# An FFN's norm statistics taken one pair later, x loaded in eight pieces on two queues, and the layer loop written out

## The reference

```
for l in range(2):
    x = x + 0.5 * swiglu(rmsnorm(x, g1[l]), w_ffn1_in[l], w_ffn1_out[l])
    x = x + mixing_sublayer(rmsnorm(x, g2[l]), ...)            # retention and forgetting attention
    x = x + 0.5 * swiglu(rmsnorm(x, g3[l]), w_ffn2_in[l], w_ffn2_out[l])
rmsnorm(x, g) = x * rsqrt(mean(x*x over the 1024 channels) + 1e-6) * g
swiglu(h)     = (silu(h @ w_in[:, :2816]) * (h @ w_in[:, 2816:])) @ w_out
```

## Time and profile before

| what | value |
|---|---|
| median of the three runs | 3042.85 us (3035.99 to 3043.49) |
| profiled execution | 3036.15 us, its span 3034.4 us |
| mean granted TensorE clock | 0.989 of full speed |
| busy: TensorE matmul, VectorE, ScalarE | 97%, 48%, 33% of the span |
| chain that ended last | TensorE 93%, VectorE 4%, ScalarE 2%, issue 1% |

### The profile page before, as it was taken

The page is one execution under the profiler, slowest core; times in us unless marked ns, Lnnn a source line. Parts: engine busy times, 40 slices in busy tenths (PEclk is TensorE's granted clock), DMA queues, the critical chain, the costliest instruction groups (busy, mean ns, idle before and its releaser), DMA issues.

```text
span 3034.4 us, 36777 instructions
## 1 busy us (share of the span) xinstructions
PE 2953.1 (97%) x13442; PEld 2378.1 (78%) x13442; DVE 1446.1 (48%) x2087; ACT 998.1 (33%) x1546; POOL 0.2 (0%) x4
## 2 busy tenths in 40 slices
PE   8999999999999999999999999999998999999996
PEld 6888887778888887888887778888887877777775
DVE  6443345555544425444255554544435445455555
ACT  3222223333322322222123233332223345434453
POOL 0000000000000000000000000000000000000000
PEclk9999999999999999999999999999999999999998
DMA  4323232212233232323232212323332121122111
GB/s 139 91 89 103 90 115 78 62 56 83 90 97 97 90 104 84 97 91 101 92 116 77 70 55 76 97 84 96 97 98 83 63 69 42 49 84 70 43 42 56
DMA packets 69368, 251.67 MB, mean 83 GB/s; under 512 B 7696, under 2 KB 7824, under 8 KB 69008
## 3 DMA queue, kind: packets, MB, share of 16 engines
q1 hardware_dynamic: 68400, 246.46, 25.8%
q10 hardware_dynamic: 864, 3.79, 0.3%
HBM read 248.13 MB, written 2.10 MB: 82 GB/s over the span
## 4 chain that ended last, share of the span: by engine, by line
PE 93%; DVE 4%; ACT 2%; issue 1%; DMA 0%; DVEq 0%; SPq 0%; ACTq 0%
PE bank L465 26%; PE bank L467 26%; PE bank L466 26%; PE bank L573 1%; PE bank L575 1%; PE bank L574 1%; PE bank L628 1%; PE bank L638 1%; PE bank L818 1%; PE bank L829 1%; PE bank L695 1%; PE bank L804 1%; PE bank L748 1%; PE bank L775 1%; PE bank L760 1%
## 5 line engine op out<-in xcount | busy, mean ns | idle before, releaser
L465 PE MATMUL bank<-xh,wh 128*128 128x512 f32 x2384 | 956.5, 401 | 16.0 <-DVE start_d L2071 9.5
L466 PE MATMUL bank<-xl,wh 128*128 128x512 f32 x2384 | 945.4, 397 | 0.0
L467 PE MATMUL bank<-xh,wl 128*128 128x512 f32 x2384 | 945.0, 396 | 0.0
L1461 DVE TENSOR_TENSOR wl<-raw,wh 128x1024 fp32r<-128x1024 f32 x460 | 561.2, 1221 | 303.6 <-ACT wh L1068 302.9
L1068 ACT ACTIVATE wh<-raw 128x1024 fp32r<-128x1024 f32 x460 | 483.4, 1052 | 398.3 <-PE bank L467 251.9
L465 PEld LDWEIGHTS bank<-xh,wh 128*128 128x128 f32 x2384 | 450.3, 189 | 127.2 <-issue 18.7
L467 PEld LDWEIGHTS bank<-xh,wl 128*128 128x128 f32 x2384 | 449.9, 189 | 109.0
L466 PEld LDWEIGHTS bank<-xl,wh 128*128 128x128 f32 x2384 | 450.3, 189 | 106.5 <-issue 1.9
L1509 DVE TENSOR_TENSOR ta<-bank,rstd 128x512 f32<-128x512 f32 x88 | 60.9, 692 | 463.3 <-PE bank L467 460.7
L467 PE MATMUL bank<-uh,wl 128*128 (+1 forms) x704 | 277.4, 394 | 0.0
L466 PE MATMUL bank<-ul,wh 128*128 (+1 forms) x704 | 276.0, 392 | 0.0
(11 more groups left out here) (355 smaller groups left out, 2832.6 us busy)
## 6 DMA issues: line engine op xcount, KB each, us to landing
raw<-stream SPq DMA_DIRECT2D x460, 512.0 KB, 3.5
x<-x_t SPq DMA_DIRECT2D x4, 512.0 KB, 8.1
dec<-decay ACTq DMA_DIRECT2D x2, 1024.0 KB, 6.3
out<-x SPq DMA_DIRECT2D x8, 256.0 KB, 2.0
rp<-rope ACTq DMA_DIRECT2D x2, 512.0 KB, 7.6
cst<-const SPq DMA_DIRECT2D x1, 708.5 KB, 10.8
ffraw<-ff_w ACTq DMA_DIRECT2D x2, 316.0 KB, 9.8
posi<-pos SPq DMA_DIRECT2D x1, 256.0 KB, 10.4
```

Source lines behind the costliest of these rows:

```text
L465: pe.matmul(o, wh[:, s, c], rhs_h, start=first, stop=False)
L466: pe.matmul(o, wh[:, s, c], rhs_l, start=False, stop=False)
L467: return pe.matmul(o, wl[:, s, c], rhs_h, start=False, stop=last)
L1461: dve.tensor_tensor(wl[:, at.slot, :], raw[:, at.raw, :], wh[:, at.slot, :].bitcast(F32), ALU.subtract).then_inc(split_lo, 1)
```

## The change

1. Start: `vecs` is loaded first, then panel 0; x comes in eight loads, tiles 2, 4, 6 on SyncE's queue and 0, 1, 3, 5, 7 on ScalarE's. ScalarE makes `xh` of the first norm, VectorE only `xl`.
2. Every FFN: `chain_col` moves into the middle of the second pair, `chain_bc` into the middle of the third. Pairs 3 and 4 are written out before TensorE's loop. Panels 4 and 5 are split in `norm_chain` (`highs`, `lows`), after `diag` and ahead of the copy of `rstd`; the first pair then splits none and the second only panel 6.
3. The first pair's banks are 4, 5 in both FFNs; the mixing sublayer's output uses banks 2, 3 instead of 2, 5.
4. The loop over the two layers is written out on TensorE, ScalarE and VectorE.

```diff
         def _(sp):
+            sp.dma_start(vecs[:], vec).then_inc(vec_in, 16)
             sp.dma_start(raw[:, 0, :], stream[0]).then_inc(raw_in[0], 16)
-            sp.dma_start(vecs[:], vec).then_inc(vec_in, 16)
-            for i in range(X_PARTS):
-                d = slice(i * KD // X_PARTS, (i + 1) * KD // X_PARTS)
-                sp.dma_start(x[:, d, :], x_in[:, d, :]).then_inc(x_part[i], 16)
-                if i == 1:
+            for d in (2, 4, 6):
+                sp.dma_start(x[:, d, :], x_in[:, d, :]).then_inc(x_part[d], 16)
+                if d == 4:
                     sp.dma_start(raw[:, 1, :], stream[1]).then_inc(raw_in[1], 16)
...
-                    if first:
+                    if first and j < 2:
                         pe.wait_ge(*resid.at(n * KD + (1 if j == 0 else KD - 1), "X"))
-                    else:
+                    elif not first:
                         pe.wait_ge(*fin.at(it - 2, "B"))
...
-                        if first and j == 1 and half == 0:
-                            chain_bc(n, 7)
-                    if first and j == 0:
-                        pe.wait_ge(const_in, 16)
-                        chain_col(n, 6)
+                        if first and half == 0:
+                            if j == 1:
+                                pe.wait_ge(const_in, 16)
+                                chain_col(n, 6)
+                            elif j == 2:
+                                chain_bc(n, 7)
...
-            with pe.Fori(0, DEPTH) as l:
+            for l in range(DEPTH):
...
+            for d in (0, 1, 3, 5, 7):
+                act.dma_start(x[:, d, :], x_in[:, d, :]).then_inc(x_part[d], 16)
             act.wait_ge(memsets, 1)
             act.activation(start_a[:], eps[:], ACT.Copy).then_inc(rg_act.sem, 1)
             high(At(0, 0), True)
-            squares(0, lambda d: d in (1, 6) and high(At(0, 1 + d // 4), True))
-            high(At(0, LEAD), True)
+            act.wait_ge(vec_in, 16)
+            for d in range(KD):
+                act.wait_ge(x_part[d], 16)
+                act.activation(xh[:, d, :], x[:, d, :], ACT.Copy, scale=vecs[:, d:d + 1]).then_inc(start_h, 1)
+                if d == 3:
+                    high(At(0, 1), True)
+            squares(0, lambda d: d in (1, 5) and high(At(0, 2 + d // 4), True))
...
                 chain_std(l * 3 + 2, 6)
+                highs(p0 + AT_FFN2, (1, 2))
...
             for d in range(KD):
                 add_squares(0, d)
-                if d == 6:
-                    low(At(0, 2))
-            low(At(0, LEAD))
+                if d in (1, 5):
+                    low(At(0, 2 + d // 4))
...
-                norm_chain(n2, 7)
-                ffn_in(l * 2 + 1, n2, p0 + AT_FFN2, FIRST_BANKS[1])
+                norm_chain(n2, 7, lambda: lows(p0 + AT_FFN2, (1, 2)))
+                ffn_in(l * 2 + 1, n2, p0 + AT_FFN2)
```

More of the change, by code:

```diff
@@ L312, in build @@
         panel_done = sem("panel_done")
-        x_part = [sem(f"x_part{i}") for i in range(X_PARTS)]
+        x_part = [sem(f"x_part{i}") for i in range(KD)]
         vec_in, const_in, pos_in = sem("vec_in"), sem("const_in"), sem("pos_in")
@@ L516, in pair @@
                         last.then_inc(panel_done, 1)
-                        if first and j == 1 and half == 0:
-                            chain_bc(n, 7)
-                    if first and j == 0:
-                        pe.wait_ge(const_in, 16)
-                        chain_col(n, 6)
-                for j in range(2):
-                    pair(j, idx + 2 * j, None, True)
-                with pe.Fori(1, KF // 2) as i:
+                        if first and half == 0:
[4 more added lines that the diff above has]
+                                chain_bc(n, 7)
+                for j in range(4):
+                    pair(j, idx + 2 * j, f * KF + j, j < 3)
+                with pe.Fori(2, KF // 2) as i:
                     for j in range(2):
@@ L1068, in high, with highs @@
                 act.activation(wh[:, at.slot, :], raw[:, at.raw, :], ACT.Copy).then_inc(split_hi, 1)
+            def highs(at, tiles):
+                for i in tiles:
+                    high(at + i + LEAD)
             def squares(n, after=None):
@@ L1084, in ffn_in, with pair @@
             def ffn_in(f, idx):
-                def pair(j, at, first):
+                def pair(j, at, splits):
                     it = f * KF + j
-                    if not first:
+                    if splits > 1:
                         high(at + LEAD)
@@ L1415, in _ @@
             act.activation(cos2[64:112, :], turn[64:112, :], ACT.Sin).then_inc(trig_act.sem, 1)
-            with act.Fori(0, DEPTH) as l:
+            for l in range(DEPTH):
                 p0 = At(l * (LAYER1 // SLOTS), 0)
@@ L1495, in diagonal, with lows @@
                                   ALU.mult).then_inc(st.sem, 1)
+            def lows(at, tiles):
+                for i in tiles:
+                    low(at + i + LEAD)
             def norm_chain(n, b, between=None):
@@ L1509, in scaled, with ffn_in, pair @@
                 dve.tensor_tensor(dst, src, rstd[:], ALU.mult).then_inc(st.sem, 1)
-            def ffn_in(f, n, idx, first_banks):
-                def pair(j, a, b, at, first=False):
+            def ffn_in(f, n, idx):
+                def pair(j, a, b, at, splits):
                     it = f * KF + j
-                    if not first:
+                    if splits > 1:
                         low(at + LEAD)
@@ L1521, in pair @@
                     dve.tensor_tensor(u32[:], sa[:], tb[:], ALU.mult).then_inc(fin.sem, 1)
-                    low(at + 1 + LEAD)
+                    if splits:
+                        low(at + 1 + LEAD)
                     dve.wait_ge(*fin_act.at(it, "UH"))
@@ L1527, in ffn_in @@
                 dve.wait_ge(*chain.at(n, "RB"))
[L1528 to L1529 removed]
+                pair(0, *(bank[i] for i in FIRST_BANKS), idx, 0)
+                pair(1, bank[2], bank[3], idx + 2, 1)
                 with dve.Fori(1, KF // 2) as i:
                     for q in range(2):
[L1532 removed]
+                        pair(i * 2 + q, bank[2 * q], bank[2 * q + 1], (idx + 2 * q).fours(i), 2)
             def ffn_out(f, n, idx):
@@ L2084, in _, with meanwhile @@
             reduced("s", ang, 0.0, "A")
-            norm_chain(0, 7, lambda: reduced("c", turn, 0.25, "s6"))
+            def meanwhile():
+                reduced("c", turn, 0.25, "s6")
+                lows(At(0, 0), (1, 2))
+            norm_chain(0, 7, meanwhile)
             dve.tensor_copy(ident16[:], ident).then_inc(mask_set, 1)
             dve.tensor_copy(masks[:], cst[:, C_CAUSAL:C_KEEP]).then_inc(mask_set, 1)
-            with dve.Fori(0, DEPTH) as l:
+            for l in range(DEPTH):
                 p0 = At(l * (LAYER1 // SLOTS), 0)
-                ffn_in(l * 2, l * 3, p0, FIRST_BANKS[0])
+                ffn_in(l * 2, l * 3, p0)
                 n = l * 3 + 1
```

36 lines of the change are left out of this document (21 added, 15 removed).

## The result

The changed kernel takes 3052.82 us (median of six runs, 3050.95 to 3054.19), the kernel before, with three more runs beside it, 3040.84 us (six runs, 3035.99 to 3043.49). The ratio is 1.0041, 95% interval 1.0028 to 1.0054: slower by 12 us, with 8.5 as the lower end. The profiled execution took 3050.95 us, its span 3049.2 us, against 3036.15 and 3034.4.

What follows compares the result with a forecast made beforehand. TensorE, busy 97% of the span, bounds the kernel. Start -1.8, layer 1's first FFN +0.9, two second FFNs +2.5 each, two clock falls +4.4 sum to +8.5: 3051 us on base 3042.85, range 3039 to 3060.

Steps and rivals of the forecast that it cites:

- the later FFNs: FFNs after the program's first: +2.5 us for each layer's second FFN, +0.9 for layer 1's first.
- the start: Program start through the first FFN: column-sum wait goes, third and fourth pairs wait; fourth pair at 52.3 against 54.09, -1.8 us.
- the clock: TensorE's clock falls behind two of the four longer new waits, 2.2 us each: +4.4 us, bounds 0 and +11.
- The fourth-pair wait: Layer 0's second FFN: TensorE's fourth pair waits 2.5 us for panel 6's split, queued behind the later broadcast and rstd copy.
- the sign: Trace sign of being right: each FFN's fourth pair's first matmul waits 2.4 to 2.6 us for `wl`, not a bank.
- Layer 1's first FFN: There the late `ta` stops mattering and the new fourth-pair wait does: fourth pair at 1213.40 against 1212.50, +0.9 us.
- rival 3: All FFNs: no fourth-pair wait; start wins 7.5 and up to 1.4, layer 1's first FFN 1.5; -10.4 us, 3032; 5%.
- The splits ahead of `rstd`: Splitting panels 4 and 5 between `diag` and the copy costs VectorE 2.4 us, hidden by 3 in layer 0's second FFN.
- Rival 1: Whole program: TensorE's clock holds through all the new waits; +4.1 us, 3047; chance 15%.
- Rival 2: Whole program: TensorE's clock falls at every new wait; +15 us, 3058; chance 12%.
- Rival 4: Start: interleaved loads hold back panel 1 until about 14.9, everything there 2.8 us later; sum +11.3, 3054; chance 8%.

Runs made afterwards that it cites:

- experiment 3: The changed kernel with two unused matmuls on TensorE ahead of each FFN's fourth pair; 3051.34 us, ratio 1.0026 to the kernel before.
- experiment 1: The changed kernel with the late sums and broadcast only in the program's first FFN, later FFNs as before the change; 3040.46 us, ratio 0.9995.
- experiment 2: The changed kernel with panel 6 also split ahead of the copy of rstd in all four FFNs; 3037.49 us, ratio 0.9990.
- experiment 4: The kernel before with only the loop over the two layers written out on TensorE, ScalarE and VectorE; 3038.83 us, ratio 0.9993.
- experiment 6: The kernel before with only the changed start: loads, xh on ScalarE, panels 2 and 3 split among the squares; 3039.99 us, ratio 0.9990.
- Experiment 5: experiment 1 plus, in the first FFN, panels 4 and 5 split ahead of the angles' second part and panel 6 behind it; 3037.00 us, ratio 0.9985.
- Experiment 8: The changed kernel with all eight x tiles loaded on SyncE's queue, panel 1 behind tile 3; 3052.30 us, ratio 1.0029.
- 11: The kernel of experiment 1 measured again without an edit in the last set of runs; 3040.72 us, ratio 0.9996.
- experiment 9: experiment 1 with three unused matmuls ahead of the fourth pair of each of the three later FFNs; 3052.11 us, ratio 1.0035.
- experiment 10: experiment 1 with one unused matmul ahead of the fourth pair of each of the three later FFNs; 3048.10 us, ratio 1.0022.
- experiment 12: experiment 1 with twelve unused matmuls ahead of the first FFN's fourth pair and none later; 3049.84 us, ratio 1.0028.

## Why the prediction was right, step by step

The forecast was 3051 us, slower by 8.5 with a 52% chance of less than 0.3% and 42% of more; measured are 3052.82 and +12.0, over that bound of 9 us and inside the range of 3039 to 3060. The mechanism of the waits was right. Of the sum, the later FFNs held, the start was too good by 1.8 us, and the clock was put in the wrong place and sized too small. How near the sum came is partly luck: take the measured 0.0 of the start, +0.4 of layer 1's first FFN and +2.4 of each second FFN from the 12.0, and 6.8 are left for the clock, an estimate, of which the falls behind the fourth pairs' waits are the smaller part (1.5 to 2 by experiment 3); the larger comes from unchanged layers, where the forecast had nothing. The forecast of 3051 also lies nearer to 3052.82 than +8.5 to +12.0 because its base, 3042.85, was 2 us above the median of six runs.

**The fourth-pair wait** (2.5 us, for `low` of panel 6, not for a bank): 2.42 us of delay at layer 0, and 2.25 or 2.26 us of idle time at all three places (the sign asked for 2.4 to 2.6), each ended by `wl`. Experiments 1 and 2 show the cause: it is gone when the broadcast is early, and also when the broadcast is late and the split stands ahead of it. The three together are 7.5 us: from the end of layer 0's mixing sublayer to layer 1's, and from there to the third layer's first norm, the repeated changed kernel needs 1159.6 + 498.56 us, experiment 1 1154.6 + 496.08, so 5.0 + 2.5 more, with no clock fall in either.

**Layer 1's first FFN** (+0.9 against before): the late `ta` of the earlier trace rows is gone. The written-out loop won 2.2 us in all in experiment 4, where the 1.5 of rival 3 stood beside "a few tenths"; so without a clock fall this FFN comes out at about +0.4, not +0.9: the repeated changed kernel needs 2.8 us more than before between the two mixing sublayers' ends (1159.6 against 1156.75), of which 2.42 are layer 0's second FFN.

**The splits ahead of `rstd`** (hidden by 3 us in the later FFNs): right. No third pair waits there.

**The start** (-1.8; 0.0 measured). The loads: panel 0's `wh` at 6.18 (6.7), panel 1's at 10.83 (12.1), first matmul at 9.93 (10.5), last sum's end at 23.83 (25.9): all sooner than forecast. What failed is the step from the start of the angles to the split of panel 4, which took only VectorE's "9.92 us of its own work" and no wait. (The 9.92 themselves were read rightly: in experiment 6, with the sums at their old place, the angles start at 23.66 and the copy of `rstd` at 33.58.) The sums now stand on TensorE's path in the second pair, at 28.69; ScalarE takes the root only after them, and loads its table first (29.72, 1.28 us); so VectorE stands still for 2.48 us at the reciprocal (31.31), with the second part of the angles and panel 4's split queued behind it. That ate the 2 us won before. The third pair came at 37.53, as forecast (37.1), but after a wait of 2.18 instead of 1.7; and the half clock behind it cost the 1.6 us or so by which the broadcast (44.78) and the fourth pair (54.13, forecast 52.3) were late. Experiment 5 removes both waits for a split at the start (0.37 us for a bank are left) by placing the splits around the angles.

The Trainium skill, "DMA: Bandwidth & Descriptors", section "Issuing engines are not separate DMA queues", said that a second issuing engine brings no bandwidth. Experiment 8 agrees in that the loads share: with one queue panel 0 was rounded at 4.89 us instead of 6.18, x's first tile was there at 6.62 instead of 4.45, and the first matmul stood at 9.39 instead of 9.93. What two queues carry in sum it does not show.

**The clock** (+4.4 by two falls of 2.2 behind the new waits). Behind the waits of 2.25 us it fell in 2 of 9 cases (the changed kernel, its repeat, experiment 8), behind the one of 2.73 at the start in 5 of 7, behind the 2.18 at the start in all 10 profiles that have it, and not behind experiment 6's 1.62; one fall cost 1.4 to 1.6 us (24 matmuls from such a row on took 7.1 to 7.3 us, and 5.7 where the clock held), not the 2.2 taken from the longer fall of the earlier trace rows. The third pair's wait, which the forecast left out of its two falls, was the surest place. Experiment 3 says what the falls at the fourth pairs are worth: about 1.5 to 2 us. More is lost in unchanged code. Against experiment 1 (with 11) the changed kernel (with its repeat) is 8.5 us later at `ckh` and needs 2.5 more from there, on the average of two profiles each: 11.0 of the 12.5 between their medians (3052.8 and 3053.3 against 3040.5 and 3040.7). Of the 8.5, 7.5 are the waits and 0.7 is the one fall behind them (1.4 in one of two profiles); 0.7 more are lost between the third layer's first column sums and `ckh`, in unchanged code, and 0.4 less up to the first mixing sublayer's end. So by the profiles the waits make three fifths of the loss, and the last two layers, whose code is the same, another 3.2 us; 1.5 us of the medians' difference no profile shows.

That these later falls come with the delay and not with the waits is shown by experiments 9 and 10, in which TensorE waits at no fourth pair of the later FFNs and the kernel loses 3.8 and 4.9 us more than the added work. Why is open. The arrival time separates the kernels of the table by their runs at the high clock, though not by their rests, and experiment 12, made to test just that, fell between: by its runs the arrival counts, by its one profile it does not. Profiles are one execution each, and no experiment set the arrival time alone.

**The rivals.** Rival 1 (clock holds, +4.1) is refuted for the program as a whole, though it describes most of the 2.25 us waits. Rival 2 (+15) was too large in its price per wait; the first profile, 14.8 over before's, is near its number by another way. Rival 3 (waits hidden) did not occur; experiments 2 and 5 are what it described, and they did not reach its 3032. Rival 4 (panel 1 late) is refuted: ScalarE had panel 1 at 10.83 us, against 10.69 before. One sentence on the range contradicts itself: 3039 to 3060 is said to leave out most of rival 2, whose 3058 lies inside.

## What to carry to other kernels

When a broadcast is moved later, look at what stands behind it in the consumer's queue: not the result but the operand splits queued behind it were late, and moving them ahead of it (experiment 2) turned the loss into nothing. A copy that waits for another engine's small result is a place to put independent work in front of, on every engine in the chain. And in a kernel whose TensorE is busy 97% of the span, a change of a few microseconds can come with as large a loss of granted clock far behind its place; compare many runs and their clocks before crediting it to the edit.

## What the hardware showed that was not expected

- The spread of one kernel from run to run goes with its clock: over 94 runs the kernel before took 3034 us at a mean granted clock of 0.990 and 3046 us at 0.985.
- An idle stretch of only 1.27 us before short matmuls of 64 columns was followed by the lower level in 17 of 28 cases, at 5 us each, more than the 1.4 us behind 2.25 us of idle time among 512-column matmuls.
- 2.6 us of added matmuls cost 7.5 us (experiment 10).
- VectorE's 2.59 us at the return of the layer loop vanish when it is written out, and 2.2 us of them are seen in the time between the two layers (experiment 4).
